# Sums of squares of the q and k norms: one fp32 pass, or two fp32r passes over the rounded squares and what the rounding left

## What is computed

```python
def rms(x):
    xf = x.astype(jnp.float32)
    return (xf * lax.rsqrt(jnp.mean(xf * xf, axis=-1, keepdims=True) + EPS)).astype(x.dtype)

z = h @ p['w_in']
# neighbourhood attention: q, k of 4 heads of 64
q, k = rms(q) * p['na_q_norm'], rms(k) * p['na_k_norm']
# latent attention: cq of 256, ckv of 192, then the heads' parts of 64 and 32
q = ((rms(cq) * p['mla_cq_norm']) @ p['mla_w_uq'])
kv = ((rms(ckv) * p['mla_ckv_norm']) @ p['mla_w_ukv'])
q_nope, q_rope, k_nope, k_rope = rms(...) * gains        # over 64, 32, 64, 32
# grouped attention: q, k of 64
q, k = rms(q) * p['gqa_q_norm'], rms(k) * p['gqa_k_norm']
```

## Time and profile before

| | us |
|---|---|
| three runs | 2322.05, 2324.03, 2324.19 (median 2324.03) |
| span of the profiled execution | 2322.3 |
| TensorE busy | 2250.2 (97%) |
| VectorE busy | 1338.5 (58%) |
| ScalarE busy | 938.6 (40%) |
| GpSimd busy | 154.4 (7%) |
| input stage of layer 0 | about 62 to 212 |
| input stage of layer 1 | about 1402 to 1522 |

### The profile page before, as it was taken

One profiled execution on the slowest core, in us unless ns is written; L12 is line 12 of the kernel. 1 busy time (PEld: TensorE's weight loads), 2 busy tenths in 40 slices (PEclk: granted clock), 3 DMA queues, 4 the chain that ended last, 5 costly groups with the idle time before them and its releaser, 6 DMA issues.

```text
span 2322.3 us, 35196 instructions
## 1 busy us (share of the span) xinstructions
PE 2250.2 (97%) x12956; PEld 1879.7 (81%) x12956; DVE 1338.5 (58%) x1958; ACT 938.6 (40%) x1387; POOL 154.4 (7%) x165
## 2 busy tenths in 40 slices
PE   6999989999999999999999989999999999999999
PEld 4789666888888878888888877777788887888887
DVE  7555576566667465435534566656655566545555
ACT  4454667422223343213312346556643334424332
POOL 0113010000000000000000002210100000000000
PEclk8999999999999999999999999999999999999999
DMA  7121010344444211111211131211055552323323
GB/s 291 55 64 64 28 41 20 110 153 136 142 137 166 73 63 64 64 64 64 64 63 59 60 129 64 70 58 59 11 172 174 170 187 76 99 92 98 97 94 118
DMA packets 58785, 221.26 MB, mean 95 GB/s; under 512 B 6752, under 2 KB 6752, under 8 KB 57904
## 3 DMA queue, kind: packets, MB, share of 16 engines
q1 hardware_dynamic: 44496, 160.46, 21.1%
q0 software_dynamic: 14176, 59.26, 7.7%
HBM read 214.45 MB, written 5.24 MB: 95 GB/s over the span
## 4 chain that ended last, share of the span: by engine, by line
PE 89%; DVE 6%; ACT 2%; issue 2%; DMA 0%; SPq 0%; DVEq 0%; ACTq 0%
PE PS L631 86%; PE PS L959 2%; DVE TM L1568 1%; DVE SM L1837 1%; ACT W_hi L1136 1%; DVE F_lo L1565 1%; DVE W_lo L1565 1%; ACT TM L1136 0%; DVE H_lo L1568 0%; ACT XY L1136 0%; DVE PS L1848 0%; DVE XY L1871 0%; DMA XY<-x_in 0%; DVE XY L1568 0%; ACT H_hi L1136 0%
## 5 line engine op out<-in xcount | busy, mean ns | idle before, releaser
L631 PE MATMUL PS<-H_hi,W_hi 128*128 128x512 f32 (+1 forms) x2256 | 805.6, 357 | 16.2 <-DVE H_lo L1568 5.9
L631 PE MATMUL PS<-H_lo,W_hi 128*128 128x512 f32 (+1 forms) x2256 | 794.0, 352 | 0.0
L631 PE MATMUL PS<-H_hi,W_lo 128*128 128x512 f32 (+1 forms) x2256 | 792.8, 351 | 0.0
L1565 DVE TENSOR_TENSOR W_lo<-W_st,W_hi 128x1024 fp32r<-128x1024 f32 x278 | 342.3, 1232 | 553.9 <-ACT W_hi L1136 552.6
L1136 ACT ACTIVATE W_hi<-W_st 128x1024 fp32r<-128x1024 f32 x278 | 293.6, 1057 | 827.5 <-PE PS L631 827.0
L631 PEld LDWEIGHTS PS<-H_hi,W_hi 128*128 128x128 f32 x2256 | 427.2, 189 | 89.2 <-issue 22.2
L631 PEld LDWEIGHTS PS<-H_lo,W_hi 128*128 128x128 f32 x2256 | 427.4, 189 | 58.5 <-issue 2.6
L631 PEld LDWEIGHTS PS<-H_hi,W_lo 128*128 128x128 f32 x2256 | 427.0, 189 | 57.7
L631 PE MATMUL PS<-F_hi,W_hi 128*128 128x512 f32 (+1 forms) x968 | 343.1, 354 | 9.6 <-DVE XY L1568 3.1
L631 PE MATMUL PS<-F_lo,W_hi 128*128 128x512 f32 (+1 forms) x968 | 340.4, 352 | 0.0
L631 PE MATMUL PS<-F_hi,W_lo 128*128 128x512 f32 (+1 forms) x968 | 339.6, 351 | 0.0
(11 more groups left out here) (131 smaller groups left out, 2009.7 us busy)
## 6 DMA issues: line engine op xcount, KB each, us to landing
W_st<-w_all SPq DMA_DIRECT2D x278, 512.0 KB, 3.5
RA<-w_mod POOLq DMA_DIRECT2D x40, 512.0 KB, 3.7
TM<-w_mod POOLq DMA_DIRECT2D x40, 512.0 KB, 3.7
FA<-w_ada SPq DMA_DIRECT2D x8, 512.0 KB, 15.7
XY<-bias_na POOLq DMA_DIRECT2D x2, 1792.0 KB, 8.1
XY<-x_in SPq DMA_DIRECT2D x4, 768.0 KB, 12.2
x_spill<-XY POOLq DMA_DIRECT2D x1, 3072.0 KB, 10.1
RA<-w_mod SPq DMA_DIRECT2D x5, 512.0 KB, 9.9
```

The lines of the kernel that those rows point to most:

```text
L631: return nc.tensor.matmul(o, lhsT, rhs, start=start, stop=stop)
L1565: return nc.vector.tensor_tensor(o, a, b, f)
```

## The change

The matrices get fp32r copies `MTR` (1/256 on all, blocks of 64, blocks for mla), made once by ScalarE in the first norm. There is no copy for 1/192: ckv uses the 1/256 matrix, and a factor 4/3 goes into its root's scale, its Newton constants and its gains. For each source ScalarE squares the raw tile twice, into `SQ` in fp32 and into `SQ_HI` in fp32r; VectorE subtracts (`square_lo`) and writes the remainder `SQ_LO` over `SQ`. `statistic` makes two fp32r matmuls where there was one in fp32, always over all 128 output partitions, and waits for `sq_lo`. A single statistic goes behind term 5, of two the first behind term 3, the second behind term 7. On VectorE `square_lo(t)` stands in the gemm event ahead of `used`, except for ckv0 (behind) and, in layer 1, nq1, whose `used` goes ahead of the stat event before. The gains are scaled by eight small operations where there were six. Cut to the core:

```diff
+R_ALL, R_64, R_MLA = range(3)
+FROM_256 = {"ckv": 4.0 / 3.0}
...
-    return [Item("ckv", [(at["ckv0"], 0, P, M_192), (at["ckv1"], 0, HD, M_192)], (0, P), T, C_CKV),
+    return [Item("ckv", [(at["ckv0"], 0, P, R_ALL), (at["ckv1"], 0, HD, R_ALL)], (0, P), T, C_CKV),
...
+        TMR = nc.alloc_sbuf_tensor_at("TMR", [P, 2, T], F32R, offset=tm_at)
...
+        MTR = sb("MTR", [P, 3, P], F32R)
...
+        SQ_HI, SQ_LO = [F_lo[:, i, :] for i in range(2)], [TMR[:, i, :] for i in range(2)]
...
-                pe.wait_ge(S["sq"], base["sq"] + c + len(it.src))
+                if i == 0:
+                    pe.wait_ge(S["mats_r"], 3)
+                pe.wait_ge(S["sq_lo"], base["sq_lo"] + c + len(it.src))
                 wait(pe, "newton", base["newton"] + 2 * i - 1 if i else 0)
-                o0, o1 = it.rows
                 for s0, sn in segs(it.w):
                     for q, (_, r0, r1, mat) in enumerate(it.src):
-                        ins = mm(pair(3)[o0:o1, s0:s0 + sn], MT[r0:r1, mat, o0:o1],
-                                 SQ[(c + q) % 2][r0:r1, s0:s0 + sn], q == 0, q == len(it.src) - 1)
+                        for half in (SQ_HI, SQ_LO):
+                            ins = mm(pair(3)[:, s0:s0 + sn], MTR[r0:r1, mat, :], half[(c + q) % 2][r0:r1, s0:s0 + sn],
+                                     q == 0 and half is SQ_HI, q == len(it.src) - 1 and half is SQ_LO)
...
-                        stop = (3 if len(due) == 1 else 2) if n == 0 else 7 if x.name == "gk" else 6
+                        stop = (5 if len(due) == 1 else 3) if n == 0 else 7
...
                 load_root_table()
+                act.wait_ge(S["const_loaded"], 16)
+                for r, m in ((R_ALL, M_256), (R_64, M_64), (R_MLA, M_MLA)):
+                    op(MTR[:, r, :], MT[:, m, :], ACT.Copy).then_inc(S["mats_r"], 1)
...
-                        op(SQ[squares % 2][r0:r1, 0:tiles[t].w], RAW[t % 4][r0:r1, 0:tiles[t].w], ACT.Square
-                           ).then_inc(S["sq"], 1)
+                        raw = RAW[t % 4][r0:r1, 0:tiles[t].w]
+                        op(SQ[squares % 2][r0:r1, 0:tiles[t].w], raw, ACT.Square)
+                        op(SQ_HI[squares % 2][r0:r1, 0:tiles[t].w], raw, ACT.Square).then_inc(S["sq"], 1)
                         squares += 1
...
-                    op(y, pair(3)[r0:r1, 0:it.w], ACT.Abs_reciprocal_sqrt, bias=EPSB[r0:r1, :]
+                    op(y, pair(3)[r0:r1, 0:it.w], ACT.Abs_reciprocal_sqrt, bias=EPSB[r0:r1, :],
+                       scale=FROM_256.get(it.to, 1.0)
                        ).then_inc(S["y0"], 1)
...
-                stt(t, m, EPS, t, ALU.add, ALU.mult).then_inc(S["newton"], 1)
+                stt(t, m, EPS * part, t, ALU.add, ALU.mult).then_inc(S["newton"], 1)
                 dve.wait_ge(S["newton"], b + 1)
-                stt(t, t, -3.0, y, ALU.add, ALU.mult).then_inc(S["newton"], 1)
+                stt(t, t, -3.0 * part, y, ALU.add, ALU.mult).then_inc(S["newton"], 1)
...
-                                (C_GK, C_MQ, 1.0), (C_MQ, C_MK, MLA_K ** -0.5), (C_MK, C_BG, 1.0)):
+                                (C_GK, C_MQ, 1.0), (C_MQ, C_MK, MLA_K ** -0.5), (C_MK, C_CKV, 1.0),
+                                (C_CKV, C_MK2, FROM_256["ckv"]), (C_MK2, C_BG, 1.0)):
...
+                def square_lo(t):
+
+                    nonlocal squares
+                    for tile, r0, r1, _ in (src for it in its for src in it.src):
+                        if tile == t:
+                            dve.wait_ge(S["sq"], base["sq"] + squares + 1)
+                            sub(SQ_LO[squares % 2][r0:r1, 0:tiles[t].w], SQ[squares % 2][r0:r1, 0:tiles[t].w],
+                                SQ_HI[squares % 2][r0:r1, 0:tiles[t].w]).then_inc(S["sq_lo"], 1)
+                            squares += 1
...
+                    if l and order[e + 1:e + 2] == [("gemm", nq1)]:
+                        used(0, 0, b0 + tiles[nq1].visit)
...
-                        if tiles[t].last:
+                        if t == 0:
+                            used(0, 0, b0 + tiles[t].visit)
+                        square_lo(t)
+                        if t and t != nq1 and tiles[t].last:
                             used(0, 0, b0 + tiles[t].visit)
```

More of the change, by code:

```diff
@@ L70 @@
 adab_loaded eps_set cb_silu mod_acc mod_fold sq_sum x_head x_reloaded x_spilled out_stored
-sq ss y0 newton norm_u norm_hi norm_lo
+sq sq_lo mats_r ss y0 newton norm_u norm_hi norm_lo
 in_raw y_sq in_zn in_hi in_lo rope_shuf rope_step kr_copy nv_copy nv_tr nv_store tok_copy
@@ L221, in mk @@
     def mk(h):
-        return Item("mk", [(at["uk%d" % h], 0, P, M_64)], (0, P), T, C_MK2, 2 * h, z=2)
+        return Item("mk", [(at["uk%d" % h], 0, P, R_64)], (0, P), T, C_MK2, 2 * h, z=2)
     def mq(h):
-        return Item("mq", [(at["uq%d" % h], 0, P, M_MLA)], (0, P), w, C_MQ, h, rope=2)
+        return Item("mq", [(at["uq%d" % h], 0, P, R_MLA)], (0, P), w, C_MQ, h, rope=2)
     def gq(t):
-        return Item("gq", [(at["gq%d" % t], 0, P, M_64)], (0, P), w, C_GQ, t, rope=0)
+        return Item("gq", [(at["gq%d" % t], 0, P, R_64)], (0, P), w, C_GQ, t, rope=0)
     def nq(t):
-        return Item("nq", [(at["nq%d" % t], 0, P, M_64)], (0, P), w, C_NAQ, t, z=len(segs(w)))
+        return Item("nq", [(at["nq%d" % t], 0, P, R_64)], (0, P), w, C_NAQ, t, z=len(segs(w)))
     def nk(t):
-        return Item("nk", [(at["nk%d" % t], 0, P, M_64)], (0, P), T, C_NAK, t, z=2)
-    return [Item("ckv", [(at["ckv0"], 0, P, M_192), (at["ckv1"], 0, HD, M_192)], (0, P), T, C_CKV),
-            Item("kr", [(at["ckv1"], 64, 96, M_MLA)], (64, 96), T, C_MK, rope=2),
-            Item("gk", [(at["gk"], 0, P, M_64)], (0, P), T, C_GK, 0, rope=0),
-            Item("cq", [(at["cq0"], 0, P, M_256), (at["cq1"], 0, P, M_256)], (0, P), w, C_CQ),
+        return Item("nk", [(at["nk%d" % t], 0, P, R_64)], (0, P), T, C_NAK, t, z=2)
+    return [Item("ckv", [(at["ckv0"], 0, P, R_ALL), (at["ckv1"], 0, HD, R_ALL)], (0, P), T, C_CKV),
+            Item("kr", [(at["ckv1"], 64, 96, R_MLA)], (64, 96), T, C_MK, rope=2),
+            Item("gk", [(at["gk"], 0, P, R_64)], (0, P), T, C_GK, 0, rope=0),
+            Item("cq", [(at["cq0"], 0, P, R_ALL), (at["cq1"], 0, P, R_ALL)], (0, P), w, C_CQ),
             gq(0), gq(1), mk(0), mk(1), nk(0), nk(1), mq(0), mq(1), nq(0), nq(1), mq(2), mq(3)]
@@ L262, in in_counts @@
     n_rope = sum(i.rope is not None for i in its)
-    return dict(sq=sum(len(i.src) for i in its), ss=len(its), y0=len(its), y_sq=len(its), newton=2 * len(its),
+    n_sq = sum(len(i.src) for i in its)
+    return dict(sq=n_sq, sq_lo=n_sq, ss=len(its), y0=len(its), y_sq=len(its), newton=2 * len(its),
                 in_raw=len(in_tiles(l)), in_zn=sum(i.z for i in its), in_hi=4, in_lo=4, rope_shuf=n_rope,
@@ L333, in hybrid_backbone_kernel @@
         RA = sb("RA", [P, 7680])
+        tm_at = -(-nc.sbuf_base // 32) * 32
         TM = sb("TM", [P, 5, T])
+        TMR = nc.alloc_sbuf_tensor_at("TMR", [P, 2, T], F32R, offset=tm_at)
         PAR, MOD = sb("PAR", [P, N_PAR]), sb("MOD", [P, 2, ADA_T + ADA_1])
@@ L1581, in used, with newton @@
                     split_lo(b % 2, i * per + (b + 3))
-            def newton(r0, r1, w, n, ss, y, t):
+            def newton(r0, r1, w, n, ss, y, t, part):
                 m, y, t = pair(3)[r0:r1, 0:w], y[r0:r1, 0:w], t[r0:r1, 0:w]
@@ L1723, in in_stage @@
                 tiles, its, b0, w = in_tiles(l), items(l), done[0], width(l)
-                z = n_lo = n_rope = 0
+                z = n_lo = n_rope = squares = 0
+                def square_lo(t):
[6 more added lines that the diff above has]
+                            squares += 1
                 def compressed_lo(i):
@@ L1735, in in_stage @@
                 order, later = events(), None
+                nq1 = next(t for t, x in enumerate(tiles) if x.name == "nq1") if l else None
                 if l:
-                    nq1 = order.index(("gemm", next(t for t, x in enumerate(tiles) if x.name == "nq1")))
-                    order[nq1 - 1], order[nq1] = order[nq1], order[nq1 - 1]
                     uq3 = order.index(("gemm", len(tiles) - 1))
                     order[uq3], order[uq3 + 1] = order[uq3 + 1], order[uq3]
-                for what, t in order:
+                for e, (what, t) in enumerate(order):
+                    if l and order[e + 1:e + 2] == [("gemm", nq1)]:
+                        used(0, 0, b0 + tiles[nq1].visit)
                     if what == "values":
@@ L1757, in in_stage @@
                     r0, r1 = it.rows
-                    newton(r0, r1, it.w, t, base["ss"] + t + 1, Y0[t % 2], RT)
+                    newton(r0, r1, it.w, t, base["ss"] + t + 1, Y0[t % 2], RT, 1.0 / FROM_256.get(it.to, 1.0))
                     for q, (tile, s0, s1, _) in enumerate(it.src):
```

2 lines of the change are left out of this document (1 added, 1 removed).

## The result

The changed kernel takes 2337.17 us (median of 4 runs, 2336.33 to 2338.09), the kernel before beside it 2323.78 (2322.05 to 2324.19): a ratio of 1.0066 with a 95% interval of 1.0054 to 1.0078. It is 13.4 us slower. The forecast had it 6.6 us slower (2330.6), with a range up to 2337. The median lies 0.2 us beyond that range, less than the four runs differ among themselves; what is off is the size of the loss, which is twice the forecast. The span of the profiled execution is 2336.1 us, 13.8 above the old one.

What follows compares the result with a forecast made beforehand. TensorE bounds the kernel, with 89% of the chain, and fills both input stages. Saving -19.2, added idle +27.2, old waits -1.9, start +0.5 make +6.6 on the 2324.03 us median: 2330.6 us, range 2319 to 2337.

Steps and rivals of the forecast that it cites:

- The saving: TensorE's statistics in both input stages: two fp32r passes for one fp32 matmul save 10.6 and 8.6, together 19.2 us.
- The stalls: Idle time put on TensorE by late squares, subtractions and splits: 12.1 us in layer 0, 15.1 in layer 1.
- block 8: gq1's W_lo split behind both its Squares and the subtraction: 2.1 us in layer 0; 0.3 in layer 1.
- statistic 12: Subtraction behind item 11's shuffle, which waits for GpSimd's rope of item 10: 2.4 us in layer 0, 3.6 in layer 1.
- What was to be taken off for the old kernel: TensorE's waits already there in the two input stages: 1.0 us in layer 0 and 0.9 in layer 1.
- The clearest case: Block 4 of layer 1: copy, Squares, subtraction and W_lo split come later, so TensorE idles 3.2 us before cq1.
- rival 2: Waits about pay for the saving if VectorE reaches subtractions before shuffles wait for ropes: 2321.1 us; 22%.
- The first step that failed: Tile-by-tile ledger of both stages: each instruction takes its row's duration, a W_lo split 1.23 us, starting when input and engine are ready.
- block 17: Layer 1, its split already last ready, now behind uq3's squares, which wait for root 13: 1.7 us.
- Rival 3: Port lock: some eight subtractions beside a rope wait and delay it, 0.9 us each: 2337.8 us; 12%.
- The second step that failed: Both input stages: TensorE's clock taken at full speed, with no term for a lower clock in the sum.
- The start: Three MT to MTR copies ahead of the first root on ScalarE delay the chain: +0.5 us.

Runs made afterwards that it cites:

- the kernel with unwaited GpSimd work: Changed kernel with rope operations cut to one column, then three full-size GpSimd multiplications for which nobody waits: 2338.94 us, ratio 1.0076.
- the two kernels without ropes: Changed kernel and kernel before, each with GpSimd's three rope operations cut to one column: 2324.6 us (ratio 1.0011) and 2323.46 us (1.0003).
- the fillers: Changed kernel plus useless matmuls ahead of four long TensorE waits (8 at three places, 14 at the fourth): 2333.11 us, ratio 1.0044.
- the one-pass kernel: Against the changed kernel: one fp32r pass over one rounded square, old places, no second Square or subtraction, remainder dropped: 2297.43 us, ratio 0.9894.
- the second order: Changed kernel with the W_lo split ahead of the subtraction on VectorE for every tile but ckv1: 2349.29 us, ratio 1.0115.

## Why the prediction was right in its direction and wrong in its size

**The saving: right.** 0.71 us a source at 768 columns for 0.70. Alone it brings 15.4 us (11.8 to 19.5) for the 18.7 reckoned.

**The stalls: right in place, some too small.** TensorE's waits came to 28.9 us, and the text said near 27. By the distance between starts, layer 0 idles 13.3 us for 12.1: statistic 4 1.8 (1.7), block 8 2.35 (2.1), statistic 6 1.4 (1.2), statistic 12 2.8 (2.4), block 16 1.6 (1.6), statistic 14 1.4 (1.25). Layer 1 idles 18.8 for 15.1. What was to be taken off for the old kernel was read too low: 1.9 us from the earlier trace rows, where all its rows make 3.1 and the distance between starts 3.5 (1.3 and 2.2). The clearest case, cq1, came out as worked; ScalarE, VectorE and TensorE there, beside the earlier trace rows:

```profile
1420.03 0.79 ACT L1145 ACTIVATE XY<-PS 128x768 f32<-128x768 f32 x1
```

```profile
1422.46 0.96 DVE L1579 TENSOR_TENSOR TMR<-TM,F_lo 128x768 fp32r<-128x768 f32 x1 [1.35 <-ACT F_lo L1145]
1423.48 1.23 DVE L1579 TENSOR_TENSOR W_lo<-W_st,W_hi 128x1024 fp32r<-128x1024 f32 x1
```

```profile
1424.80 0.47 PE L638 MATMUL PS<-H_hi,W_hi 128*128 128x512 f32 x1 [2.90 <-issue]
```

Copy 2.5 us later (0.8 of it from the later start of the stage; 1.55 was forecast), subtraction, split, and cq1 3.04 us late (3.2 forecast).

Statistic 12 too was 3.9 late (3.6), with the wait of item 11's shuffle for GpSimd as in the earlier trace rows. But the number fits better than the reason. The forecast made that wait the cause; in the kernel with unwaited GpSimd work it is gone, and statistic 12 still comes 3.4 late, while without GpSimd's work it comes 1.3 late. What holds it up is VectorE's work beside GpSimd's, and the wait only takes its place.

The late shuffle rules out rival 2, which needed item 11's shuffle done before 1502; it ran at 1510.28:

```profile
1510.25 0.01 DVE L1822 LOAD_MASK_SELECT TM<-FA  x1 [1.23 <-POOL FA L564]
1510.28 0.71 DVE L1822 STREAM_SHUFFLE TM<-FA 32x512 f32<-32x512 f32 x1
1511.02 0.69 DVE L1579 TENSOR_TENSOR TMR<-TM,F_lo 128x512 fp32r<-128x512 f32 x1
```

**The first step that failed: each operation given the duration of its row, a W_lo split 1.23.** That put the ropes in once, at block 8 of layer 0. The missed stalls of layer 1 lie at block 8 (2.0 us for 0.3) and block 5 (0.9 for nothing), 2.6 us together; block 17 has 2.24 for 1.7. Without ropes neither block 5 nor block 8 of layer 1 has a wait, and block 17 has the same 2.2. At block 8, VectorE and GpSimd:

```profile
1449.89 1.49 DVE L1579 TENSOR_TENSOR TMR<-TM,F_lo 128x512 fp32r<-128x512 f32 x1 [0.44 <-ACT F_lo L1145]
1451.31 2.29 DVE L1579 TENSOR_TENSOR W_lo<-W_st,W_hi 128x1024 fp32r<-128x1024 f32 x1
```

```profile
1449.53 1.30 POOL L561 TENSOR_TENSOR TM<-TM,ROPE 128x512 f32<-128x512 f32 x1 [7.11 <-DVE TM L1822]
1450.78 1.74 POOL L562 TENSOR_TENSOR RA<-RA,ROPE 128x512 f32<-128x512 f32 x1
1452.59 2.14 POOL L564 TENSOR_TENSOR RA<-RA,TM 128x512 f32<-128x512 f32 x1
```

A shuffle starts a rope; the subtraction and the split that now stand behind the shuffle run beside it, one after the other, and each is longer by up to the rest of a GpSimd operation: 1.49 for 0.69, 2.29 for 1.23. The old order had a wait for W_hi in that place more often, 30.1 us of them for 10.6, and a loss ahead of a wait costs nothing.

**Rival 3: nearly the right time, and not for its reason.** It gave 2337.8 with 12%, for 2337.17 measured. But it charged the subtractions, and named as its sign that they average well over 1.0 us. They average 974 ns at 768 columns in layer 0 and 770 at 512 in layer 1, for 0.96 and 0.68. The splits behind them paid, as did the Newton steps in the kernel with unwaited GpSimd work. The sign that I named would have spoken against a rival whose mechanism was at work. So the two kernels without ropes lie 1.1 us apart, and the ropes are the 14 that are left.

**The second step that failed, and the larger: the clock, put at nothing.** The ledger took TensorE's pace as constant. Four of the long waits were followed by some 4 us at a granted clock of 0.53 to 0.60: 6.8 us by the starts, 5.5 by the fillers. Some 3 of the ropes' 14 us are this. The old kernel had no wait over 0.6 us in these stages, so its trace of them couldn't show it; but a ledger with waits of 2 and 3 us in it should have asked.

**The start: wrong.** It was to cost 0.5 us. The three copies cost 0.2 us each as said, but the root ran earlier, not later (beside the earlier trace rows):

```profile
25.47 0.69 ACT L1145 ACTIVATE MTR<-MT 128x128 fp32r<-128x128 f32 x3
26.07 0.88 ACT L1145 ACTIVATE TM<-PS,SM 128x768 f32<-128x768 f32 x1
```

and TensorE's low clock near 40 us was shorter (0.76 over 37 to 45 us, where the old one has 0.53 over 38 to 47). That shorter stretch is what the 2.7 us go with. In the fourteen profiled executions the first tile of layer 0 starts at 60.6 to 61.6 us in the ten whose mean granted clock over 25 to 50 us is 0.80, at 63.0 to 63.5 in the three with 0.73, and at 64.5 in the one with 0.66. The three with 0.73 are both kernels without the copies and the one-pass kernel, which has them; the first root comes at 25.7 to 28.1 us in the kernels with copies and at 26.7 and 26.9 in the two without. The whole time moves with the clock in the same way in one and the same kernel: the executions of the kernel before at a mean of 0.998 took 2318.9 and 2319.4 us, those at 0.994 took 2323.6 to 2324.4. So the -2.7 can't be put down to the change, and by it the measured loss came out nearer to the forecast than the stages did: that part is luck. Why the low clock lasts longer in one execution than in another, no run shows.

**The balance.** 6.6 forecast; -3.2 for the start, +1.2 and +3.7 for the idle time, -1.6 for the old kernel's idle time (3.5 by the same measure, for 1.9), +1.7 and +5.1 for the clock: 13.5, against 13.8 by the spans. Idle time by the distance between starts is read to about 0.1 us at each of some 25 places.

## What to carry to other kernels

On an engine that works in line, charge an added operation not with its own length but with what it moves: the operation behind it may lose a gap in which a known slowdown had cost nothing. Where VectorE and GpSimd both read SBUF, lay their operations side by side on one timeline and let them exclude each other, since that can cost more than the added work itself: 14 us here, where the subtractions without ropes cost some 7 (2324.6 less the 2317.89 with two Squares and no subtraction). And on top of a wait of 2 us or more that is put into a stage in which TensorE was always busy, the clock may cost some 1.7 us more; here it did so behind four of six such waits.

## What the hardware showed that I had not expected

- The clock falls inside a stage that TensorE fills to 88% and more: after idle times of 2.35, 2.0, 3.9 and 2.2 us the granted clock is 0.53 to 0.60 over the next 3.4 to 4.3 us, after others of 3.04 and 2.83 it isn't. What TensorE did around each isn't enough in these traces to say which it will be. The 2.83 at statistic 12 of layer 0 was followed by 1.00 in one execution, and about the same wait by 0.57 in the kernel with the fillers. Useless matmuls in the waits won back 5.5 of 2338.6 us.
- The ropes are worth 14 us in the changed kernel and nothing that shows in the old one, though they slow its Newton steps too (836 ns for 692). Taking GpSimd's dependences away and leaving its work changed nothing (2338.94 for 2338.6).
- The price moves to whoever is second behind the shuffle: the split 2.29 for 1.23 in one order, the subtraction 2.02 for 0.96 in the other, and the second order is 10.7 us slower, because the statistic is wanted sooner.
